# Hyena bias added as one-row matmuls, imaginary filter spectra before real ones, filter norm split around the first spectrum

## The chip, the cores and the metric

One core of one Trainium2 chip runs the whole kernel. The metric is the device time of one execution in microseconds (us); lower is better. The engines are TensorE (PE; its weight loads are PEld), VectorE (DVE), ScalarE (ACT), GpSimd (POOL) and SyncE (SP), which here only issues DMAs.

## What is computed

A transformer-like layer over 1024 latent tokens and 256 context tokens of width 1024: modulation from a condition vector, a joint input projection, three mixers side by side (Hyena long convolution, neighbourhood attention, RG-LRU), an output projection and a SwiGLU feed-forward block. The change touches only how the Hyena filters are prepared:

```python
h = jnp.sin(f_freq[0] * (z @ f_w1 + f_b1))
h = jnp.sin(f_freq[1] * (h @ f_w2 + f_b2))
k = (h @ f_w3).reshape(L, 2, 2, HY_WIDTH) * jnp.exp(-t * deltas)
k_circ = jnp.concatenate([kf, zeros, kb[:0:-1]], axis=0)
k_circ = k_circ / jnp.sum(jnp.abs(k_circ), axis=0, keepdims=True)
k_f = jnp.fft.rfft(k_circ, axis=0)
...
z = gate * (fft_conv(z, k_f[:, n]) + hy_bias[n] * z)
```

The bias term `hy_bias * z` is the same as adding a constant to every real value of the filter's spectrum, or adding it to the filter's tap at time 0.

## The kernel before

All products are made at close to full float32 precision from three passes over rounded halves: head of the weights times head of the data (`w_hi`, `eo_hi`), head times rest (`eo_lo`) and rest times head (`w_lo`). A head is a copy to the type f32r (ACT), a rest is a subtraction (POOL, some on DVE).

**Taps.** The filter is held as 8 tiles (`TILE[0..7]`, the first is tile 0) of even and odd parts, 128 x 2 x 512 each, in `eo`. For each pair of tiles PE multiplies (`taps`, L1942), DVE applies the decay (`window_taps`, L1342), ACT takes absolute values into `kabs` (L771) and makes the head of the tile (`filter_head`, L762), DVE takes the larger of the even and odd part (`larger`, L1328, into `kmax`), PE sums that over all taps into bank 5 (`filter_norm`, L2029; two records each), and POOL or DVE makes the rest (L1167, `tap_rest` L1334: DVE has the rests at positions 1, 3 and 5 of `SPLIT`, which are `TILE[2]`, `TILE[4]` and `TILE[6]`). Tile 0 needs a repair of its first row first (`efix`, L1355 and L1356, signal `k_fix`), and has its head and rest last.

**Bias.** When all eight norms are in bank 5, DVE multiplies the bias row by the norm (L1376), adds it to the first row of tile 0 (L1377, signal `k_bias`) and forms the row `nrow` of the norm for the later scaling (L1378, signal `nrow_ok`). Only then does ACT make the head of tile 0 and POOL its rest.

**Spectra.** `spectrum(n)`, n = 0 to 7, multiplies a table of cosines (n even: real part) or sines (n odd: imaginary part) with all 8 tiles, 24 matmuls of 128x512 in the order of `SPLIT`: heads (L1958), tap rests (L1967), table rests (L1974); for n = 0 the last two are exchanged. The table chunk n comes from memory by `k_raw(n)` (L522) into one of two `raw` buffers, ACT makes its head (`k_head(n)`, L754), POOL its rest (`k_rest(n)`, L1154). The result leaves by `spectrum_copy` (ACT, L810), `spectrum_out` (DVE, L1423) and `spectrum_store` (SP, L548).

**What lies between them.** PE also does `mod_sums(0..3)` (L1999, the modulation, whose weights `ada` are four loads of 2 MB), `norm_columns` (L1991, four tiny matmuls on `nrow`), `mod_columns` (L2007) and, from before `spectrum(3)` on, `turn_input` (L2020), the transposes of the normalised tokens. ACT squares the token tiles (`mean_square(n)`, L724), each of which is loaded by ACT's own DMA queue into `xstat`, three buffers deep: `mean_square(n)` issues the load of tile n + 3 (L717). It scales the tokens by their norm (`normalise(n)`, L796), which wants the rx values made from all ten squares.

Every engine runs one list of instructions, written out by hand in its block, with semaphores between them. SP's list in this part is: small loads, `k_raw(0)`, `k_raw(1)`, the four `ada` loads (L527), the bias table of the attention written through memory (`rpad` L529 and L531, sixteen copies to `rskew` L534), `k_raw(2)`, six token tiles (L540), `k_raw(3)`, `spectrum_store(0)` and so on. ACT's list around the point in question is `spectrum_copy(1)`, `k_head(3)`, `normalise(0..3)`, `spectrum_copy(2)`.

Of the kernel before, what the change touches and what calls it, by code (L numbers as in the profile page):

```python
# [17 lines left out]
F32 = mybir.dt.float32  # L18
F32R = mybir.dt.float32r
# [5 lines left out]
P = 128  # L25
# [23 lines left out]
RAD = 8  # L49
TAPS = ((0, 0), (1, 2), (1, 0), (1, 3), (1, 1), (0, 3), (0, 1), (0, 2))  # L50
TILE = tuple(4 * par + i for par, i in TAPS)
SPLIT = tuple(k for k in TILE if k) + (0,)
DVE_SPLIT = (1, 3, 5)
TURNS = ((0, 2), (2, 6), (6, 10))
PLUS, MINUS = (0, 7, 1, 6), (4, 3, 5, 2)
GU_JOBS, DOWN_JOBS = 2 * FT, 24
# [105 lines left out]
def program(nc, A, out):  # L162
    ctx = ExitStack()
    with ctx:
        base = 16512

        def at(name, off, shape, dt=F32):
            return nc.alloc_sbuf_tensor_at(name, [P] + list(shape), dt, offset=base + off)
# [29 lines left out]
        efix = at("efix", H_ + 20480, [2 * HY])  # L198
        nrow = efix
        kmax = [at(f"kmax{r}", a, [2 * HY]) for r, a in enumerate((H_ + 22528, H_ + 24576, H_ + 8192))]  # L200
        kabs = [at("kabs0", H_, [2, 2 * HY]), at("kabs1", H_ + 4096, [2, 2 * HY])]
        arow = at("arow", H_ + 26624, [2, HALF])
        zf = at("zf", H_, [SEQ])
# [258 lines left out]
        def _(sp):  # L462
# [55 lines left out]
            def k_raw(n):  # L518

                if n >= 2:  # L520
                    sp.wait_ge(klo, n - 1)
                sp.dma_start(raw[:, n % 2, :], A["ktab"][:, n * SEQ:(n + 1) * SEQ]).then_inc(kraw_ld[n % 2], 16)  # L522

            k_raw(0)
            k_raw(1)
# [15 lines left out]

            def spectrum_store(n):

                m, ri = n // 2, n % 2
                sp.wait_ge(kv_ok, n + 1)
                for side, j in enumerate((PLUS[m], MINUS[m])):
                    for o in range(2):
                        sp.dma_start(spec[o, j, :, ri, :], kev[:, n % 2, side, o * HY:(o + 1) * HY]).then_inc(ks_out[n % 2], 16)  # L548
# [149 lines left out]
        def _(act):  # L698
# [20 lines left out]
            def mean_square(n):  # L719

                if n:
                    act.wait_ge(x_sq, n)
                act.wait_ge(xs_ld[n % 3], 16 * (n // 3 + 1))
                act.activation(xstat[n % 3][:], xstat[n % 3][:], ACT.Square, accum_out=ssq[:, n:n + 1]).then_inc(x_sq, 1)  # L724
                if n + 3 < len(TILES):
                    act.wait_ge(x_sq, n + 1)
                    stats_dma(n + 3)
# [21 lines left out]
            def k_head(n):  # L749

                act.wait_ge(kraw_ld[n % 2], 16 * (n // 2 + 1))
                if n >= 2:
                    act.wait_ge(kjob, n - 1)
                act.activation(w_hi[:, n % 2, :], raw[:, n % 2, :], ACT.Copy).then_inc(khi, 1)  # L754

            k_head(0)
            mean_square(0)
            mean_square(1)

            def filter_head(k):  # L760

                act.activation(eo_hi[:, k].rearrange("p x c -> p (x c)"), eo[:, k].rearrange("p x c -> p (x c)"), ACT.Copy).then_inc(e_hi, 1)  # L762

            for t in range(RAD):
                if t:
                    act.wait_ge(k_eo, 4 * (t // 2) + 3 + t % 2)
                else:
                    act.wait_ge(k_fix, 1)
                if t >= 2:
                    act.wait_ge(k_max, t - 1)  # L770
                act.activation(kabs[t % 2][:], eo[:, TILE[t]], ACT.Abs).then_inc(k_abs, 1)  # L771
                if TILE[t]:
                    filter_head(TILE[t])
            k_head(1)
            mean_square(2)
            mean_square(3)

# [27 lines left out]
            def spectrum_copy(n):  # L805

                act.wait_ge(kjob, n + 1)
                if n:
                    act.wait_ge(kv_rd, n)
                act.activation(ktmp[:], ps[:, 2 * (n % 2), :], ACT.Copy).then_inc(kc_ok, 1)  # L810

            act.wait_ge(k_bias, 1)
            filter_head(0)
            mod_rows(0)
            mod_rows(1)
            mean_square(4)
            mean_square(5)
            mean_square(6)
            spectrum_copy(0)
            k_head(2)  # L820
            mean_square(7)
# [301 lines left out]
        def _(pool):  # L1123
# [25 lines left out]
            def k_rest(n):  # L1149

                pool.wait_ge(khi, n + 1)
                if n >= 2:
                    pool.wait_ge(kjob, n - 1)
                pool.tensor_tensor(w_lo[:, n % 2, :], raw[:, n % 2, :], w_hi[:, n % 2, :].bitcast(F32), ALU.subtract).then_inc(klo, 1)  # L1154
# [6 lines left out]
                    pool.tensor_tensor(ha_lo[:, k, a * P:z * P], xm[:, k, a * P:z * P], ha_hi[:, k, a * P:z * P].bitcast(F32),  # L1161
                                       ALU.subtract).then_inc(x_lo, 1)

            for n, k in enumerate(SPLIT):
                if n not in DVE_SPLIT:
                    pool.wait_ge(e_hi, n + 1)
                    pool.tensor_tensor(eo_lo[:, k].rearrange("p x c -> p (x c)"), eo[:, k].rearrange("p x c -> p (x c)"),  # L1167
                                       eo_hi[:, k].bitcast(F32).rearrange("p x c -> p (x c)"), ALU.subtract).then_inc(e_lo, 1)
                if n in (3, 6):
                    k_rest(n // 6)  # L1170
            k_rest(2)
            k_rest(3)
            k_rest(4)
# [85 lines left out]
        def _(dve):  # L1259
# [69 lines left out]

            def tap_rest(n):  # L1330

                k = SPLIT[n]
                dve.wait_ge(e_hi, n + 1)
                dve.tensor_tensor(eo_lo[:, k].rearrange("p x c -> p (x c)"), eo[:, k].rearrange("p x c -> p (x c)"),  # L1334
                                  eo_hi[:, k].bitcast(F32).rearrange("p x c -> p (x c)"), ALU.subtract).then_inc(e_lod, 1)
# [27 lines left out]
            for p in range(1, RAD // 2):  # L1363
                window_taps(p, 0)
                larger(2 * p - 2)
                window_taps(p, 1)
                larger(2 * p - 1)
                if p >= 2:
                    tap_rest(2 * p - 3)
            larger(RAD - 2)  # L1370
            larger(RAD - 1)
            tap_rest(5)

            dve.wait_ge(k_acc, RAD)
            dve.wait_ge(par_ld, 16 * 17)
            link(dve.tensor_tensor(hrow[0:1, :], hrow[0:1, :], ps[0:1, 5, :], ALU.mult))  # L1376
            dve.tensor_tensor(eo[0:1, 0], eo[0:1, 0], hrow[0:1, :].unsqueeze(1).broadcast_to([1, 2, 2 * HY]), ALU.add).then_inc(k_bias, 1)  # L1377
            dve.tensor_scalar(nrow[0:1, :], ps[0:1, 5, :], float(SEQ), None, ALU.mult).then_inc(nrow_ok, 1)  # L1378

            def lam_series():  # L1380
# [44 lines left out]
                dve.nop().then_inc(kv_rd, 1)  # L1425
                dve.nop().then_inc(kv_ok, 1)

            lam_series()
            filter_scale()
            spectrum_out(0)  # L1430
            dve.wait_ge(x_sq, 10)
            dve.tensor_scalar(rx[:], ssq[:], 1.0 / D, EPS, ALU.mult, ALU.add).then_inc(x_rs, 1)
            dve.wait_ge(x_sqrt, 1)
# [467 lines left out]
        def _(pe):  # L1901
# [43 lines left out]

            def spectrum(n):

                x = n % 2
                pe.wait_ge(khi, n + 1)
                if n >= 2:  # L1950
                    pe.wait_ge(kv_rd, n - 1)
                bank = lambda k: ps[:, 2 * x + k // 4, :]

                def heads():
                    for i, k in enumerate(SPLIT):
                        if n == 0:
                            pe.wait_ge(e_hi, i + 1)
                        pe.matmul(bank(k), w_hi[:, x, k * P:(k + 1) * P], eo_hi[:, k, x, :], start=k in (SPLIT[0], SPLIT[4]), stop=False)  # L1958

                def tap_rests(last):  # L1960
                    for i, k in enumerate(SPLIT):
                        if n == 0:
                            if i in DVE_SPLIT:
                                pe.wait_ge(e_lod, DVE_SPLIT.index(i) + 1)
                            else:
                                pe.wait_ge(e_lo, i + 1 - sum(d < i for d in DVE_SPLIT))
                        ins = pe.matmul(bank(k), w_hi[:, x, k * P:(k + 1) * P], eo_lo[:, k, x, :], start=False,  # L1967
                                        stop=last and k in (SPLIT[3], SPLIT[7]))
                    return ins

                def table_rests(last):
                    pe.wait_ge(klo, n + 1)
                    for k in SPLIT:
                        ins = pe.matmul(bank(k), w_lo[:, x, k * P:(k + 1) * P], eo_hi[:, k, x, :], start=False,  # L1974
                                        stop=last and k in (SPLIT[3], SPLIT[7]))
                    return ins

                heads()
                if n == 0:
                    table_rests(False)  # L1980
                    ins = tap_rests(True)
                else:
                    tap_rests(False)
                    ins = table_rests(True)
                ins.then_inc(kjob, 1)
# [45 lines left out]
            for p in range(RAD // 2):  # L2031
                taps(p, 0)
                taps(p, 1)
                if p >= 2:
                    filter_norm(2 * p - 4)
                    filter_norm(2 * p - 3)
            for t in range(RAD - 4, RAD):
                filter_norm(t)
            pe.wait_ge(sil_ok, 1)
            mod_sums(0)  # L2040
            mod_sums(1)
            spectrum(0)
            norm_columns()
            mod_columns(0)
            mod_columns(1)
# [353 lines left out]
```

## Time and profile before

| | us |
|---|---|
| median of 3 runs | 1478.46 (1477.99 to 1478.96) |
| profiled execution, own time | 1482.41 |
| its span | 1480.4 |
| mean granted TensorE clock in it | 0.984 |

The profiled execution is some 4 us longer than the median of the others. Busy time is counted per engine; a PE that is busy nearly all the span sets the time wherever it has no hole, and what counts for this change are the first 118 us, where PE still waits for other engines and for DMAs.

### The profile page before, as it was taken

The numbers are of one execution on the slowest core, as the hardware profiler recorded it, in microseconds if no ns is written. First come the engines' busy times: TensorE is split into PE (matmuls) and PEld (weight loads), VectorE is DVE, ScalarE is ACT, GpSimd is POOL, SyncE is SP. The second block draws the span as 40 slices with busy tenths as digits, with TensorE's granted clock in tenths as the row PEclk, the third lists the DMA queues.
The fourth block names the chain that finished last, engine by engine and source line by source line (L and its number), as shares of the span: only waits on it lengthen the run. The fifth ranks groups of instructions, "written<-read, shape, count | busy, mean of one in ns | idle before, by whom it ended". The sixth has DMA issues, their size and how long they took to land.

```text
span 1480.4 us, 20446 instructions
## 1 busy us (share of the span) xinstructions
PE 1413.7 (95%) x7737; PEld 1156.2 (78%) x7737; DVE 724.8 (49%) x1022; ACT 550.1 (37%) x861; POOL 608.2 (41%) x291
## 2 busy tenths in 40 slices
PE   5989999999998999999999999999999999999997
PEld 1579667899986888778678888878877888887886
DVE  7664557893936887448875111133356121110122
ACT  4572543322315777634322222222222222223222
POOL 2362112160426553474344444444443444443442
PEclk9999999999999999999999999999999999999999
DMA  9762101414104545432323333333323433332332
GB/s 335 256 221 60 40 29 40 132 32 140 45 27 112 142 131 145 143 98 87 127 78 93 96 98 90 99 89 93 102 86 110 117 99 92 99 92 79 93 96 89
DMA packets 236447, 156.63 MB, mean 106 GB/s; under 512 B 10531, under 2 KB 221873, under 8 KB 236251
## 3 DMA queue, kind: packets, MB, share of 16 engines
q1 hardware_dynamic: 234387, 148.70, 33.2%
q10 hardware_dynamic: 1992, 6.99, 1.4%
q8 instruction: 46, 0.75, 0.2%
q14 instruction: 22, 0.18, 0.0%
HBM read 147.25 MB, written 8.81 MB: 105 GB/s over the span
## 4 chain that ended last, share of the span: by engine, by line
PE 81%; DVE 9%; SPq 3%; ACT 2%; DMA 2%; issue 2%; POOL 1%; DVEq 0%; ACTq 0%
PE ps L1909 33%; PE ps L1914 17%; PE ps L2070 11%; PE ps L2073 5%; PE ps L2230 2%; PE ps L2207 2%; PE ps L2168 2%; PE ps L2086 1%; SPq L527 1%; DMA rpad<-zpad 1%; PE ps L2115 1%; PE ps L2127 1%; DMA raw<-in_ktab 1%; PE ps L2210 1%; POOL hb_lo L1226 1%
## 5 line engine op out<-in xcount | busy, mean ns | idle before, releaser
L1127 POOL TENSOR_TENSOR w_lo<-raw,w_hi 128x1024 fp32r<-128x1024 f32 x152 | 371.4, 2443 | 473.1 <-ACT w_hi L704 473.1
L1909 PE MATMUL ps<-hb_hi,w_hi 128*128 128x512 f32 x768 | 303.8, 396 | 10.1 <-DVE g_t L1812 5.4
L1909 PE MATMUL ps<-hb_lo,w_hi 128*128 128x512 f32 x768 | 301.9, 393 | 0.0
L704 ACT ACTIVATE w_hi<-raw 128x1024 fp32r<-128x1024 f32 x152 | 160.1, 1053 | 178.5 <-PE ps L1914 171.6
L1914 PE MATMUL ps<-hb_hi,w_lo 128*128 128x512 f32 x768 | 194.0, 395 | 0.0
L1147 POOL TENSOR_TENSOR w_lo<-raw,w_hi 128x1024 fp32r<-128x1024 f32 x21 | 88.1, 4197 | 226.6 <-ACT w_hi L860 226.6
L1909 PEld LDWEIGHTS ps<-hb_hi,w_hi 128*128 128x128 f32 x768 | 145.7, 190 | 44.6 <-DVE hb_lo L1777 7.6
L1914 PEld LDWEIGHTS ps<-hb_hi,w_lo 128*128 128x128 f32 x768 | 145.9, 190 | 32.7 <-issue 2.5
L1909 PEld LDWEIGHTS ps<-hb_lo,w_hi 128*128 128x128 f32 x768 | 146.0, 190 | 29.8
L2070 PE MATMUL ps<-ha_hi,w_hi 128*128 128x512 f32 (+2 forms) x432 | 164.2, 380 | 3.7 <-ACT w_hi L860 3.4
L2070 PE MATMUL ps<-ha_lo,w_hi 128*128 128x512 f32 (+2 forms) x432 | 161.6, 374 | 0.0
L1909 PE MATMUL ps<-a_hi,w_hi 128*128 128x512 f32 x352 | 138.0, 392 | 2.0 <-ACT w_hi L704 2.0
L1909 PE MATMUL ps<-a_lo,w_hi 128*128 128x512 f32 x352 | 137.2, 390 | 0.0
L1075 ACT ACTIVATE a_hi<-a_f 128x512 f32 (+1 forms) x44 | 27.8, 632 | 209.4 <-DVEq L1817 209.4
L1815 DVE SCALAR_TENSOR_TENSOR a_f<-g_t,ps 128x512 f32<-128x512 f32 x44 | 30.2, 688 | 149.8 <-PE ps L1914 149.6
L2073 PE MATMUL ps<-ha_hi,w_lo 128*128 128x512 f32 (+2 forms) x432 | 98.9, 371 | 0.0
L2070 PEld LDWEIGHTS ps<-ha_hi,w_hi 128*128 128x128 f32 x432 | 82.1, 190 | 17.8 <-issue 7.0
L1812 DVE SCALAR_TENSOR_TENSOR g_t<-g_t,ps 128x512 f32<-128x512 f32 x44 | 30.3, 688 | 125.8 <-ACT g_t L1071 125.1
L2070 PEld LDWEIGHTS ps<-ha_lo,w_hi 128*128 128x128 f32 x432 | 82.1, 190 | 10.2
L2073 PEld LDWEIGHTS ps<-ha_hi,w_lo 128*128 128x128 f32 x432 | 80.1, 188 | 10.1
L1914 PE MATMUL ps<-a_hi,w_lo 128*128 128x512 f32 x352 | 87.6, 389 | 0.0
L1909 PEld LDWEIGHTS ps<-a_hi,w_hi 128*128 128x128 f32 x352 | 66.2, 188 | 16.4 <-ACT w_hi L704 2.8
(279 smaller groups left out, 2088.1 us busy)
## 6 DMA issues: line engine op xcount, KB each, us to landing
raw<-in_ffn_w_gu SPq DMA_DIRECT2D x88, 512.0 KB, 3.8
ada1x<-in_ada_w SPq DMA_DIRECT2D x32, 512.0 KB, 3.9
raw<-in_ffn_w_down SPq DMA_DIRECT2D x32, 512.0 KB, 4.1
raw<-in_w_in SPq DMA_DIRECT2D x22, 512.0 KB, 4.0
ada<-in_ada_w SPq DMA_DIRECT2D x4, 2048.0 KB, 21.9
raw<-in_w_out SPq DMA_DIRECT2D x16, 512.0 KB, 4.2
raw<-in_ffn_w_down SPq DMA_DIRECT2D x16, 384.0 KB, 3.5
raw<-in_ktab SPq DMA_DIRECT2D x8, 512.0 KB, 6.4
```

What stands on the lines that cost most here:

```text
L704: act.activation(w_hi[:, b, :], raw[:, b, :], ACT.Copy).then_inc(hi_done, 1)
L1127: pool.tensor_tensor(w_lo[:, b, :], raw[:, b, :], w_hi[:, b, :].bitcast(F32), ALU.subtract).then_inc(lo_done, 1)
L1147: pool.tensor_tensor(w_lo[:, b, :], raw[:, b, :], w_hi[:, b, :].bitcast(F32), ALU.subtract).then_inc(llo, 1)
L1812: dve.scalar_tensor_tensor(g_t[:], g_t[:], 1.0, ps[:, 0, :], ALU.add, ALU.mult).then_inc(acc_free, 1)
L1815: dve.scalar_tensor_tensor(a_f[:], g_t[:], 0.5, ps[:, 1, :], ALU.mult, ALU.mult).then_inc(acc_free, 1)
L1909: pe.matmul(dst, w_hi[:, b, k * P:(k + 1) * P], x, start=start and i_ == 0 and n == 0, stop=False)
L1914: ins = pe.matmul(dst, w_lo[:, b, k * P:(k + 1) * P], rhs(k)[0], start=False, stop=stop and k == nk - 1)
L2070: pe.matmul(dst, w_hi[:, b, k * P:(k + 1) * P], x[:, k, a:z], start=k == 0 and n == 0, stop=False)
L2073: ins = pe.matmul(dst, w_lo[:, b, k * P:(k + 1) * P], ha_hi[:, k, a:z], start=False, stop=k == KT - 1)
L2168: ins = pe.matmul(dst, q_[hh, 4 * rb + cb, :], rhs, start=i == 0, stop=i == 2)
L2207: pe.transpose(ps[0:m, 4 + e, c * P:(c + 1) * P], pr[:, b, e, a:a + m], ident[:])
L2230: ins = pe.matmul(ps[hh, 7, 0:P], vtm[0:m, hp, tile, hh], pT[0:m, b, e, c, :], start=c == 0, stop=c == 4)
```

## The change

The bias is no longer added to tile 0. Instead DVE splits the row bias x norm into a head and a rest (`hb_row`), and each real spectrum gets two extra matmuls with a one-row stationary operand of ones (`one_row`) and these rows. The imaginary spectra, which have no bias, come first within the pairs (`PART`): n = 0, 2, 4, 7 are imaginary, n = 1, 3, 5, 6 real. Tile 0 is treated in turn with the others. The norms of the last two tiles are summed behind `spectrum(0)`, those of tiles 4 and 5 between `mod_sums(0)` and `mod_sums(1)`. POOL makes the two first table rests ahead of all tap rests; DVE makes its three tap rests behind the last decay; ACT makes `k_head(1)` early; `mean_square(4..6)` no longer stand behind the wait for `k_bias`; `lam_series` (27 small DVE operations) stands behind `spectrum_out(0)`.

```diff
-SPLIT = tuple(k for k in TILE if k) + (0,)
-DVE_SPLIT = (1, 3, 5)
+DVE_SPLIT = (2, 4, 6)
+PART = (1, 0, 1, 0, 1, 0, 0, 1)
@@ SP, k_raw(n) and spectrum_store(n)
-                sp.dma_start(raw[:, n % 2, :], A["ktab"][:, n * SEQ:(n + 1) * SEQ]).then_inc(kraw_ld[n % 2], 16)
+                sp.dma_start(raw[:, n % 2, :], A["ktab"][:, (n - n % 2 + PART[n]) * SEQ:(n - n % 2 + PART[n] + 1) * SEQ]).then_inc(kraw_ld[n % 2], 16)
-                m, ri = n // 2, n % 2
+                m, ri = n // 2, PART[n]
@@ ACT
             k_head(0)
+            k_head(1)
             mean_square(0)
             mean_square(1)
...
-                if TILE[t]:
-                    filter_head(TILE[t])
-            k_head(1)
+                filter_head(TILE[t])
             mean_square(2)
             mean_square(3)
...
-            act.wait_ge(k_bias, 1)
-            filter_head(0)
             mod_rows(0)
             mod_rows(1)
             mean_square(4)
             mean_square(5)
             mean_square(6)
+            act.wait_ge(k_bias, 1)
             spectrum_copy(0)
@@ POOL
-            for n, k in enumerate(SPLIT):
+            k_rest(0)
+            k_rest(1)
+            for n, k in enumerate(TILE):
                 if n not in DVE_SPLIT:
...
-                if n in (3, 6):
-                    k_rest(n // 6)
@@ DVE
-                if p >= 2:
-                    tap_rest(2 * p - 3)
+            tap_rest(2)
             larger(RAD - 2)
+            tap_rest(4)
             larger(RAD - 1)
-            tap_rest(5)
-
+            tap_rest(6)
+
+            dve.wait_ge(k_eo, 4 * RAD // 2)
+            link(dve.tensor_copy(one_row[0:1, :], ones[0:1, :]))
             dve.wait_ge(k_acc, RAD)
             dve.wait_ge(par_ld, 16 * 17)
             link(dve.tensor_tensor(hrow[0:1, :], hrow[0:1, :], ps[0:1, 5, :], ALU.mult))
-            dve.tensor_tensor(eo[0:1, 0], eo[0:1, 0], hrow[0:1, :].unsqueeze(1).broadcast_to([1, 2, 2 * HY]), ALU.add).then_inc(k_bias, 1)
+            link(dve.tensor_copy(hb_row[0][0:1, :], hrow[0:1, :]))
+            dve.tensor_tensor(hb_row[1][0:1, :], hrow[0:1, :], hb_row[0][0:1, :].bitcast(F32), ALU.subtract).then_inc(k_bias, 1)
...
-            lam_series()
             filter_scale()
             spectrum_out(0)
+            lam_series()
@@ PE, spectrum(n); all of its loops run over TILE in place of SPLIT
+                    if r == 0:
+                        pe.wait_ge(k_bias, 1)
+                        for row in hb_row:
+                            pe.matmul(bank(0), one_row[0:1, :], row[0:1, :], start=False, stop=False)
@@ PE, its list
-            for t in range(RAD - 4, RAD):
-                filter_norm(t)
             pe.wait_ge(sil_ok, 1)
             mod_sums(0)
+            filter_norm(RAD - 4)
+            filter_norm(RAD - 3)
             mod_sums(1)
+            pe.wait_ge(k_eo, 2 * RAD)
             spectrum(0)
+            filter_norm(RAD - 2)
+            filter_norm(RAD - 1)
             norm_columns()
```

## Rows read from the trace of the kernel before

**Rows 1.** The page: the span of the profiled execution

```profile
span 1480.4 us, 20446 instructions
```

**Rows 2.** The chain that ended last: start, length, what (us)

```profile
27.45 15.53 DMA rpad<-zpad
...
45.25 0.63 SPq L534
...
56.39 0.46 SPq L522
...
60.81 13.73 DMA raw<-in_ktab
...
105.17 2.03 issue
```

**Rows 3.** Timeline of PE: start, length, line, tiles, shape, count, idle before

```profile
33.45 2.15 PE L2029 MATMUL ps<-kmax,ones 128*128 128x512 f32 x4
40.52 6.84 PE L2029 MATMUL ps<-kmax,ones 128*128 128x512 f32 x8 [4.93 <-DVE kmax L1328]
47.30 3.64 PE L1999 MATMUL ps<-ada,silp 128*32 128x512 f32 x32
50.87 2.33 PE L1958 MATMUL ps<-eo_hi,w_hi 128*128 128x512 f32 x8
...
56.79 0.40 PE L1991 MATMUL ps<-ident,efix 1*128 1x1 f32 x4
57.12 1.95 PE L2007 MATMUL ps<-selc,arow 128*128 128x2 f32 x16
...
73.62 1.98 PE L1974 MATMUL ps<-eo_hi,w_lo 128*128 128x512 f32 x8
77.84 1.06 PE L2020 MATMUL ps<-ident,xin 128*128 128x128 f32 x8 [2.24 <-ACT xin L796]
...
109.57 3.03 PE L1958 MATMUL ps<-eo_hi,w_hi 128*128 128x512 f32 x8
```

**Rows 4.** Timeline of ACT and of its DMA queue (ACTq)

```profile
42.07 1.04 ACT L762 ACTIVATE eo_hi<-eo 128x1024 fp32r<-128x1024 f32 x1
...
54.68 0.33 ACTq L717 DMA_DIRECT2D xstat<-in_x  x1
...
74.56 1.06 ACT L754 ACTIVATE w_hi<-raw 128x1024 fp32r<-128x1024 f32 x1 [3.80 <-DMA raw<-in_ktab]
75.52 4.25 ACT L796 ACTIVATE xin<-xin,rx 128x1024 f32<-128x1024 f32 x4
...
90.76 0.60 ACT L810 ACTIVATE ktmp<-ps 128x512 f32<-128x512 f32 x1
```

**Rows 5.** DMAs from 56 to 76 us, ACT's queue: packets, MB, share

```profile
q10 hardware_dynamic: 419, 1.52, 22.6%
```

**Rows 6.** Windows: PE, PEld, DVE, ACT, POOL busy, PEclk, DMA share, GB/s

```profile
42.00:44.00 2.00, 2.00 (x3) 0.50 (x2) 2.00 (x3) 2.00 (x4) 0.00 (x0) 0.50 0.02 6
...
72.00:74.00 2.00, 2.00 (x10) 1.65 (x9) 0.61 (x4) 0.00 (x0) 0.00 (x0) 1.00 1.05 381
...
108.00:110.00 2.00, 2.00 (x12) 2.00 (x11) 1.75 (x4) 0.54 (x2) 1.39 (x1) 0.55 0.03 12
```

**Rows 7.** Timeline of DVE in the taps and behind them

```profile
21.92 0.67 DVE L1355 TENSOR_TENSOR efix<-eo 1x512 f32<-1x512 f32 x1
...
27.02 2.31 DVE L1328 TENSOR_TENSOR kmax<-kabs 128x512 f32<-128x512 f32 x1
...
34.34 3.38 DVE L1334 TENSOR_TENSOR eo_lo<-eo,eo_hi 128x1024 fp32r<-128x1024 f32 x1
...
41.59 0.68 DVE L1328 TENSOR_TENSOR kmax<-kabs 128x512 f32<-128x512 f32 x1
...
47.40 0.68 DVE L1376 TENSOR_TENSOR hrow<-hrow,ps 1x512 f32<-1x512 f32 x1 [1.49 <-PE ps L2029]
```

**Rows 8.** Timeline of POOL, 15 to 49 us

```profile
26.42 2.36 POOL L1167 TENSOR_TENSOR eo_lo<-eo,eo_hi 128x1024 fp32r<-128x1024 f32 x1 [24.45 <-ACT eo_hi L762]
```

More of the change, by code:

```diff
@@ L200, in program @@
         kmax = [at(f"kmax{r}", a, [2 * HY]) for r, a in enumerate((H_ + 22528, H_ + 24576, H_ + 8192))]
+        hb_row = [at("hb_row0", H_ + 8192, [2 * HY], F32R), at("hb_row1", H_ + 3072, [2 * HY], F32R)]
+        one_row = at("one_row", H_ + 18432, [P], F32R)
         kabs = [at("kabs0", H_, [2, 2 * HY]), at("kabs1", H_ + 4096, [2, 2 * HY])]
@@ L1330, in tap_rest @@
             def tap_rest(n):
-                k = SPLIT[n]
+                k = TILE[n]
                 dve.wait_ge(e_hi, n + 1)
@@ L1946, in spectrum @@
             def spectrum(n):
-                x = n % 2
+                x, r = n % 2, PART[n]
                 pe.wait_ge(khi, n + 1)
@@ L1954, in heads @@
                 def heads():
-                    for i, k in enumerate(SPLIT):
+                    for i, k in enumerate(TILE):
                         if n == 0:
                             pe.wait_ge(e_hi, i + 1)
-                        pe.matmul(bank(k), w_hi[:, x, k * P:(k + 1) * P], eo_hi[:, k, x, :], start=k in (SPLIT[0], SPLIT[4]), stop=False)
+                        pe.matmul(bank(k), w_hi[:, x, k * P:(k + 1) * P], eo_hi[:, k, r, :], start=i < 2, stop=False)
+                    if r == 0:
+                        pe.wait_ge(k_bias, 1)
+                        for row in hb_row:
+                            pe.matmul(bank(0), one_row[0:1, :], row[0:1, :], start=False, stop=False)
                 def tap_rests(last):
-                    for i, k in enumerate(SPLIT):
+                    for i, k in enumerate(TILE):
                         if n == 0:
@@ L1966, in tap_rests @@
                                 pe.wait_ge(e_lo, i + 1 - sum(d < i for d in DVE_SPLIT))
-                        ins = pe.matmul(bank(k), w_hi[:, x, k * P:(k + 1) * P], eo_lo[:, k, x, :], start=False,
-                                        stop=last and k in (SPLIT[3], SPLIT[7]))
+                        ins = pe.matmul(bank(k), w_hi[:, x, k * P:(k + 1) * P], eo_lo[:, k, r, :], start=False,
+                                        stop=last and k in (TILE[4], TILE[7]))
                     return ins
@@ L1972, in table_rests @@
                     pe.wait_ge(klo, n + 1)
-                    for k in SPLIT:
-                        ins = pe.matmul(bank(k), w_lo[:, x, k * P:(k + 1) * P], eo_hi[:, k, x, :], start=False,
-                                        stop=last and k in (SPLIT[3], SPLIT[7]))
+                    for k in TILE:
+                        ins = pe.matmul(bank(k), w_lo[:, x, k * P:(k + 1) * P], eo_hi[:, k, r, :], start=False,
+                                        stop=last and k in (TILE[4], TILE[7]))
                     return ins
```

## The prediction

> **What bounds the kernel now.** I read the page first for the span [rows 1], then the chain of waits, which says what released the work at each moment, then the timelines of PE, ACT and DVE over the first 118 us, and last the DMA windows. From the chain [rows 2] the reader is to see that the early part hangs on SP's queue: the write of `zpad` lands only at 42.98 us (behind the `ada` loads), sixteen copies of about 0.6 us each are issued from 45.25 on, so `k_raw(2)` goes out at 56.39 and `k_raw(3)` at 60.81. That chunk needs until 74.5 to land; then ACT does `k_head(3)` and, behind it in its list, `normalise(0)` and `(1)` [rows 4]: 74.56 + 0.96 + 2 x 1.06 = 77.6, and PE's first transpose starts at 77.84. I call that moment T. PE's timeline [rows 3] is a second chain into T: from the two `mod_sums` at 47.30 it has no hole until `spectrum(2)` ends at 75.60, and it waits 2.24 us there. Behind T PE runs without a hole to 105.17 and waits 2.03 us for ACT [rows 2]. All that follows is started by progress of the kernel, not by a fixed time, so what T gains is carried to the end, unless the hole at 105 us gives or takes something.
>
> So T is the later of two times: PE's, with 2.24 us to spare, and that of the DMA. Both have to move for a gain.
>
> **PE's chain.** The start S of `spectrum(0)` is 50.87 now [rows 3]. After the change there stand directly before it `filter_norm(5)` and `mod_sums(1)`; the norms of tiles 6 and 7 come behind. A norm is 2.15 / 2 = 1.08 us, a `mod_sums` 3.64 / 2 = 1.82 [rows 3]. The start is set by `larger(5)`, which ends at 41.59 + 0.68 = 42.3 now [rows 7]. In front of it goes the tap rest of 3.38 us. Against this come: the head of tile 0 on ACT, 0.95 us from start to start (rows like the head of another tile, 1.04 busy [rows 4]); its rest on POOL, 2.36 [rows 8]; and the two table rests of the same length, which POOL does from the end of `k_head(0)`, about 19.3, to about 24.1. The rows say that this is not free: a `kmax` operation beside a POOL rest takes 2.31 where one alone takes 0.68, and it ends when the POOL operation ends (26.42 + 2.36 = 28.78, plus 0.68 is 29.4) [rows 7, 8]. `efix`, at 21.92 now [rows 7], would thus end at about 24.7, 2 us later, and so would `k_fix` and the first absolute values. Following the alternation DVE, ACT, POOL for all eight tiles with these durations, and with each two-input DVE operation held until the POOL operation beside it ends, I get the end of `larger(5)` at 41.7: three rests on POOL collide with a `larger` each, and the 3.38 us that leave DVE pay for it. Bounds: 39 (no collision) to 44 (each collision 1 us worse).
>
> (The Trainium skill, SBUF — State Buffer, section SBUF: two separate sides, says that VectorE with two SBUF inputs and GpSimd take one pair of ports as an exclusive lock for a whole instruction. By that rule, which speaks against moving the table rests ahead, the collisions are whole operations, as the trace shows with 2.31 against 0.68; without the lock `larger(5)` would end near 39.)
>
> S = 41.7 + 1.08 + 1.82 = 44.6. `spectrum(0)` takes 56.79 - 50.87 = 5.92, so it ends at 50.5; its last tap rest (DVE, about 48.1) is then there. The other two norms: 52.7. Now there is a new wait: `norm_columns` needs `nrow`, and DVE forms that only now, by the product (0.68 [rows 7]), a copy of the row (the trace has no such one; between 0.35, half of that, and 0.68; I take 0.5), a subtraction and the norm row (0.68 each): 2.6 with the gaps. POOL rests in this time. So `norm_columns` starts at 55.3 against 56.79: of the 6.3 us that S gains, 1.5 are left. From there to the end of `spectrum(2)` it is 75.60 - 56.79 = 18.8 now; `spectrum(1)` is real and gets two more matmuls. Their price: 1.98 us for 8 [rows 3], thus 0.25 each, 0.5 together. A one-row f32r matmul of 512 columns is not in the trace; from below it is nothing, from above that of a norm, 1.08. PE is ready for T at 55.3 + 18.8 + 0.5 = 74.6 (76.9 with `larger(5)` at its upper bound, which makes 1478.0; at its lower one the DMA side decides).
>
> `lam_series` moves from in front of `spectrum_out(0)` to behind it. It takes about 7 us, would run from 58.5 to 66, and the ACT square it precedes is done at about 66.6: hidden. With that cover gone it would delay `normalise`, by at most 1 us.
>
> **The DMA side.** SP's issue times do not move: the waits for `zpad` and for sixteen issues are untouched, and what `k_raw(2)`, the token tiles and `k_raw(3)` wait for is earlier anyway. What moves are the loads of `xstat` tiles 7, 8 and 9 on ACT's queue. The first is issued at 54.68 and the others 1.6 us apart, because `mean_square(4..6)` stand behind `k_bias`; all 1.52 MB of them pass after 56 us [rows 4, 5], in the stretch in which the DMA engines are full (share 1.05 with 381 GB/s at 72 to 74 [rows 6]). After the change ACT makes the last absolute value and head from 41.7 to 43.6, does two squares with their loads (1.8 us each) and two row copies (0.5 each) to 48.4, and issues the three loads at about 50, 51.8 and 53.5, before `k_raw(2)`. What comes before chunk 3 is 8 x 0.524 = 4.2 MB on SP's queue. Taking 1.2 to 1.5 MB away at 0.39 MB per us saves 3.1 to 3.9 us: chunk 3 lands at 70.6 to 71.4. T by this side is 3.3 later, 73.9 to 74.7. ACT itself is ready: it stood idle for 3.80 us before `k_head(3)` for this load alone [rows 4], and what it does before that starts no later than now.
>
> So T goes from 77.84 to about 74.7: 3.1 us.
>
> **Behind T.** Real spectra n = 3, 5 and 6 have 0.5 us more each. That of n = 3 delays `spectrum(4)` and so `spectrum_copy(4)` at 90.76, which ACT takes up the moment PE ends; ACT had 0.1 to 0.2 us of slack there, so 0.3 us goes on the path. Those of n = 5 and 6 fall into the 2.03 us hole, where ACT is late and not PE: cost nothing, and 1.0 us each with the other if that hole were not there. Sum: 3.1 - 0.3 = 2.8. The sum is against the profiled time of 1482.41; the median of the runs lies 3.95 lower, and I take the same difference from it: 1478.46 - 2.8 = 1475.7. Adding a part for the chance that the hole at 105 us stops costing clock (below), I would shade to 1475.4; as the likeliest case I give 1475.5.
>
> **The rivals.**
>
> *Clock lost in the new hole.* From 52.7 to about 57.4 PE would do nothing but tiny matmuls. After the hole of 4.93 us before 40.52 [rows 3] the granted clock is 0.50 (42 to 44), after that at 105 it is 0.55 (108 to 110) [rows 6]. If it falls here, the next two `mod_sums` run at 1.2 GHz; at the second fall `spectrum(7)`'s heads took 3.03 for about 2.1 [rows 3], and with the transposes before them 1.8 us went. The same here: PE ready at 76.3, gain 1.2, time 1477.3. For it: the hole is of the length that did it; against: the matmuls at 57.12 [rows 3] were preceded by no fall now. (The Trainium skill, TensorE: Matmul & The Clock Gate, section HAM oscillation, warns that an idle array drops to half clock and pays to come back. By that rule, with which the row at 108 us agrees, this rival would be the rule and not the exception.) Chance 0.2.
>
> *Clock regained at 105 us.* PE is 1 us later against ACT there, so the hole shrinks from 2.03 to about 1.1. If the clock then stays, the 1.8 us come on top: 1475.5 - 1.8 = 1473.7. Chance 0.22.
>
> *The chunk does not land earlier, and it ends slower.* If `xstat` is not what holds chunk 3, T stays at 77.84 and PE, ready at 74.6, stands idle for 3.3 instead of 2.24 us. Then 0.3 is lost for n = 3, and if the clock falls in that longer hole, `spectrum(3)` loses 1.8: 1478.8 to 1480.6. It decides from a landing later than 74.2. For it: three more requests queue behind chunk 3 in that stretch and may share the engines with it; against: 1.52 MB at 0.39 per us is 3.9 us, which has to go somewhere. Chance 0.13.
>
> *My likeliest case*, 1475.5, own range 1474.5 to 1477: chance 0.45.
>
> **How the numbers follow.** A measurement of this kernel can tell about 0.2%, 3.0 us, from no change; the bound for faster is 1475.5, in the middle of the likeliest case. Faster: 0.22 + 0.26 of 0.45 = 0.48. Same: 0.19 + 0.20 + 0.03 = 0.42. Slower: 0.10. The range runs from 1472.9 (regained clock, with the collisions at their lower bound) to 1479.0, and leaves out the part of the slower rival in which the clock falls, and more than one gain together.
>
> **What the new profile would show.** `spectrum(0)` starting at 44 to 46 and `norm_columns` at 55 to 56; a PE hole of 2.6 us before it; `xstat` issues before 54; `k_head(3)` starting at 70.5 to 71.5; the first transpose at 74 to 75.5; `spectrum(7)`'s heads 3.0 or 2.1 us long. The prediction is wrong if `k_head(3)` still starts at 74.5, if one-row matmuls take 1 us, or if the clock reads 0.5 between 56 and 66 us.

## The result, and the profile after

| | us |
|---|---|
| changed kernel, median of 12 runs | 1482.45 (1480.93 to 1484.17) |
| kernel before, median of 12 runs beside them | 1478.62 (1476.67 to 1479.79) |
| ratio, with 95% interval | 1.0028 [1.0019, 1.0037] |
| profiled execution of the changed kernel, own time / span | 1483.53 / 1481.7 |

The change makes the kernel slower by 0.2 to 0.4%, some 4 us. I had forecast 3 us in the other direction. The page [rows 1]:

```profile
span 1481.7 us, 20465 instructions
```

PE's timeline after, with the columns of [rows 3]:

```profile
45.12 2.11 PE L1961 MATMUL ps<-eo_hi,w_hi 128*128 128x512 f32 x8
...
50.69 1.88 PE L2036 MATMUL ps<-kmax,ones 128*128 128x512 f32 x4
55.16 0.48 PE L1998 MATMUL ps<-ident,efix 1*128 1x1 f32 x4 [2.59 <-DVE efix L1381]
55.56 3.58 PE L2014 MATMUL ps<-selc,arow 128*128 128x2 f32 x16
59.07 5.15 PE L2006 MATMUL ps<-ada,silp 128*32 128x512 f32 x32
64.15 2.10 PE L1961 MATMUL ps<-eo_hi,w_hi 128*128 128x512 f32 x8
66.19 0.73 PE L1965 MATMUL ps<-hb_row,one_row 1*128 1x512 f32 x2
66.85 2.09 PE L1974 MATMUL ps<-eo_lo,w_hi 128*128 128x512 f32 x8
...
77.89 1.04 PE L2027 MATMUL ps<-ident,xin 128*128 128x128 f32 x8
...
85.09 1.04 PE L2027 MATMUL ps<-ident,xin 128*128 128x128 f32 x8
```

Up to the fourth row I read what I had forecast: `spectrum(0)` at 45.12 (44.6), a wait of 2.59 us (2.6), `norm_columns` at 55.16 (55.3). Then comes the loss: the sixteen matmuls of `mod_columns` take 3.58 us where they took 1.95 [rows 3], and the 32 of `mod_sums` 5.15 where they took 3.64. T, the first transpose, is at 77.89 and no longer waits for ACT: PE itself is late. The last row, the next transposes, serves to price the one-row matmuls further down. The windows show the clock (columns as in [rows 6]):

```profile
54.00:56.00 2.00, 0.84 (x6) 0.83 (x7) 1.10 (x2) 0.60 (x1) 0.00 (x0) 0.84 0.98 273
...
60.00:62.00 2.00, 2.00 (x16) 0.51 (x12) 1.66 (x11) 0.65 (x1) 0.00 (x0) 0.50 0.92 375
...
108.00:110.00 2.00, 2.00 (x19) 1.92 (x17) 1.31 (x3) 1.35 (x2) 0.57 (x1) 1.00 0.00 0
```

The granted clock falls about when the wait ends (the 0.84 of the first row means some 0.6 us at half clock before 56) and stands at 0.50, that is 1.2 GHz, past 62 us, for 6.8 us in all; at 108 us it is 1.00 where [rows 6] had 0.55. The chain that ended last now holds neither SP nor a DMA here, as [rows 2] did, but DVE and PE (start, length, what):

```profile
49.12 3.55 issue
52.66 0.69 DVE hrow L1378
...
59.14 5.08 PE ps L2006 x32
```

ACT's timeline answers to [rows 4]. The loads of `xstat` are issued at 49.52 and 53.02 (first and last of three), and `k_head(3)` at 71.28 waited for no chunk: ACT stood idle until PE had ended `spectrum(1)`, copied that, and went on.

```profile
49.52 0.33 ACTq L719 DMA_DIRECT2D xstat<-in_x  x1
...
70.79 0.60 ACT L811 ACTIVATE ktmp<-ps 128x512 f32<-128x512 f32 x1 [2.15 <-PE ps L1981]
71.28 1.05 ACT L756 ACTIVATE w_hi<-raw 128x1024 fp32r<-128x1024 f32 x1
```

From 56 to 76 us ACT's queue moved this, for the 1.52 MB of [rows 5]:

```profile
q10 hardware_dynamic: 101, 0.35, 4.3%
```

DVE's timeline, beside [rows 7], shows the collisions. POOL's two table rests ran from 20.19 to 24.87 (last row; POOL's own timeline), beside the first of DVE's two operations.

```profile
22.65 2.76 DVE L1355 TENSOR_TENSOR efix<-eo 1x512 f32<-1x512 f32 x1
...
39.98 2.17 DVE L1328 TENSOR_TENSOR kmax<-kabs 128x512 f32<-128x512 f32 x1
```

```profile
20.19 4.68 POOL L1154 TENSOR_TENSOR w_lo<-raw,w_hi 128x1024 fp32r<-128x1024 f32 x2 [18.21 <-ACT w_hi L756]
```

### The profile page after: what moved, and what is told of

Same layout as the page of the kernel before. It is cut to its first block, busy times and chain, and to the rows that moved or that the text cites. A ratio compares the mean times of both kernels' runs of the same rounds, so it can differ in the third digit from the quotient of the medians.

```text
span 1481.7 us, 20465 instructions
## 1 busy us (share of the span) xinstructions
PE 1417.4 (96%) x7745; PEld 1157.1 (78%) x7745; DVE 728.2 (49%) x1024; ACT 550.2 (37%) x861; POOL 607.6 (41%) x291
## 4 chain that ended last, share of the span: by engine, by line
PE 81%; DVE 12%; ACT 3%; issue 2%; POOL 1%; DMA 0%; ACTq 0%; DVEq 0%
PE ps L1912 32%; PE ps L1917 16%; PE ps L2080 11%; PE ps L2083 5%; PE ps L2240 2%; PE ps L2178 1%; PE ps L2217 1%; PE ps L2096 1%; ACT pr L995 1%; PE ps L2137 1%; PE ps L2125 1%; DVE a_f L1748 1%; PE ps L1974 1%; PE ps L1961 1%; PE ps L1981 1%
## 5 line engine op out<-in xcount | busy, mean ns | idle before, releaser
L2080 PEld LDWEIGHTS ps<-ha_hi,w_hi 128*128 128x128 f32 x432 | 82.8, 192 | 18.1 <-issue 7.0
```

The source lines that it names most:

```text
L2080: pe.matmul(dst, w_hi[:, b, k * P:(k + 1) * P], x[:, k, a:z], start=k == 0 and n == 0, stop=False)
```

## The experiments

Two theories stood at the start. **Clock:** the new wait costs the granted clock, and that costs more than the norms' move gains. **Baseline:** the 3.1 us that T was to gain were a property of one profile. Two rivals: POOL's table rests in front of the taps cost the time, or the one-row matmuls do. Each time is the median of twelve runs, given against the median of the kernel before timed beside them (35 or 22 runs); only the two profiles of experiment 2 are one run each. Warm means at a granted clock of 1.00, cold at 0.50.

**1. The kernel before, unchanged.**

> The kernel before, unchanged, for a second profile and more times. Theory A (the changed kernel loses because its own PE chain grew: clock fall behind the new hole, and one-row matmuls): this profile looks like the first, k_head(3) at 74.5 and first transpose at 77.8. Theory B (the first profile of before was an unusually slow execution, 4 us over the median, and showed the load of table chunk 3 later than it usually lands): k_head(3) starts 1 to 3 us earlier here, the first transpose at 75.7 to 77, the span near 1477.

1480.09 against 1479.98, ratio 1.0009 [0.9997, 1.0021]. Its span is 1476.0, and its profile differs from the one I had read. ACT, then PE:

```profile
72.27 1.06 ACT L754 ACTIVATE w_hi<-raw 128x1024 fp32r<-128x1024 f32 x1 [1.63 <-DMA raw<-in_ktab]
```

```profile
59.00 5.34 PE L1999 MATMUL ps<-ada,silp 128*32 128x512 f32 x32
...
77.13 1.03 PE L2020 MATMUL ps<-ident,xin 128*128 128x128 f32 x8
...
83.47 1.04 PE L2020 MATMUL ps<-ident,xin 128*128 128x128 f32 x8
...
105.77 0.41 PE L2020 MATMUL ps<-ident,xin 128*128 128x128 f32 x2 [1.34 <-issue]
```

Chunk 3 was there 2.3 us sooner than in [rows 4], T had no wait for ACT in front of it, and `mod_sums` shows the clock fall (5.34 for 3.64) that I thought absent before.

**2. Two more profiles of the kernel before.**

> The kernel before, unchanged, a third profile. Theory B (the first profile showed the load of table chunk 3 later than usual): k_head(3) starts at 70 to 73, the first transpose at 75.7 (PE ready, warm clock) to 77.2 (clock fall at 59 us), the projection at 113.7 to 115.3. If the first profile was the rule: 74.5, 77.8 and 116.5 to 118.3.

> The kernel before, unchanged, a fourth profile; expectations as for the third.

1479.63 and 1478.01, spans 1477.6 and 1475.9. The first of them had its `mod_sums` warm, and T with it:

```profile
59.40 3.64 PE L1999 MATMUL ps<-ada,silp 128*32 128x512 f32 x32
...
75.84 1.03 PE L2020 MATMUL ps<-ident,xin 128*128 128x128 f32 x8
```

The second is like experiment 1, with 5.34 and T at 77.08. So T of the kernel before is 75.84 with a warm `mod_sums` and 77.1 with a cold one, set by PE both times. The 77.84 and the 2.24 us of waiting in [rows 3] came in one profile of four. So did the slow stretch at 105 us: from T to the first matmul of the projection it took 40.5 us there and 38.1 in the three others. Of these 2.4 us, 0.7 is a longer wait (2.03 us for 1.34) and some 1.6 are slow clock behind it.

**3. Chunk 3 asked for earlier, in the kernel before.** This moves the DMA side alone.

```diff
                 x_dma(n)
+            k_raw(3)
             sp.wait_ge(ada_mm, 2)
...
             x_dma(5)
-            k_raw(3)
             spectrum_store(0)
```

> The kernel before with k_raw(3) issued ahead of the token tiles 4 and 5. If the load of chunk 3 holds the first transpose in before as the first profile shows (2.24 us of idle PE): 2.2 us faster than before, ratio 0.9985. Theory B (in the usual execution it lands in time): no change, ratio 1.000 within 0.0003.

1479.65 against 1479.98, ratio 1.0000 [0.9986, 1.0014]. T is at 75.84, and ACT's row is this:

```profile
69.54 1.05 ACT L754 ACTIVATE w_hi<-raw 128x1024 fp32r<-128x1024 f32 x1
```

`k_head(3)` is 1.8 to 3.3 us earlier than in experiments 1 and 2, and T is where PE's chain puts it: `mod_sums` start at 57.70 and T follows 18.1 us later, as in experiment 1 (59.00 and 77.13). So an earlier chunk gains nothing at T in this profile. The whole profile runs 1.1 us ahead of that of experiment 1 from the start of the taps on, which makes its T as early as the 75.84 above. The times alone say less: the twelve fall in two groups of six, at 1475.8 to 1478.4 and at 1480.9 to 1482.9, and the interval only just excludes the 2.2 us that I had set as the other outcome.

**4. The norms of the last two tiles back in front of `spectrum(0)`.** The row for DVE is then made under `spectrum(0)`.

```diff
-            spectrum(0)
             filter_norm(RAD - 2)
             filter_norm(RAD - 1)
+            spectrum(0)
             norm_columns()
```

> The changed kernel with the norms of tiles 6 and 7 summed ahead of spectrum(0) again. Theory A: spectrum(0) starts 3.9 us later (49.0) but norm_columns follow at once at 54.9 with a warm clock, so 3 us less up to mod_sums(3): 1479.3 to 1480. Theory C: no change, 1482.5.

1479.32 against 1479.98, ratio 0.9998 [0.9986, 1.0009]. PE:

```profile
46.87 1.12 PE L2036 MATMUL ps<-kmax,ones 128*128 128x512 f32 x2 [1.61 <-DVE kmax L1328]
...
53.39 0.40 PE L1998 MATMUL ps<-ident,efix 1*128 1x1 f32 x4
53.72 1.95 PE L2014 MATMUL ps<-selc,arow 128*128 128x2 f32 x16
55.60 3.64 PE L2006 MATMUL ps<-ada,silp 128*32 128x512 f32 x32
...
74.02 1.07 PE L2027 MATMUL ps<-ident,xin 128*128 128x128 f32 x8 [0.91 <-ACT xin L797]
```

`spectrum(0)` starts 2.3 us later than in the changed kernel (47.43), but everything behind it runs warm, and T is 3.9 us earlier. Of these, 1.0 belongs to the execution and not to the edit: DVE's first decay operation starts at 18.83 here and at 19.80 in the changed kernel.

**5. The wait filled by other work of the kernel.** `mod_sums(2)` and `mod_columns(0)` go ahead of `norm_columns`; `filter_scale` waits for the larger count.

```diff
             filter_norm(RAD - 1)
-            norm_columns()
+            mod_sums(2)
             mod_columns(0)
+            norm_columns()
             mod_columns(1)
-            mod_sums(2)
             mod_sums(3)
@@ DVE, filter_scale
-                dve.wait_ge(mod_done, 6)
+                dve.wait_ge(mod_done, 10)
```

> The changed kernel with mod_sums(2) and mod_columns(0) in the hole of PE behind the last two norms, norm_columns behind them. Theory A: the hole of 2.6 us and the clock fall go (3.1 us of longer tiny matmuls and mod_sums, and 2.6 of idle time); PE is ready for the first transpose at about 72.5, which then starts with the DMA side at about 74.4: 3 us faster than the changed kernel, 1479.3. If the hole costs nothing (theory C: it is the load that sets the start of the transposes, and the loss comes later): 1482.5, as the changed kernel.

1479.22 against 1479.98, ratio 1.0002 [0.9989, 1.0015]. Inside the time is dealt out otherwise: PE is early at T, waits there, and pays clock there. ACT, then PE:

```profile
73.12 1.06 ACT L756 ACTIVATE w_hi<-raw 128x1024 fp32r<-128x1024 f32 x1 [4.14 <-DMA raw<-in_ktab]
```

```profile
76.40 1.51 PE L2027 MATMUL ps<-ident,xin 128*128 128x128 f32 x8 [3.64 <-ACT xin L797]
77.56 3.35 PE L1961 MATMUL ps<-eo_hi,w_hi 128*128 128x512 f32 x8
```

From T to the projection this takes 41.0 us, for 39.3 in the changed kernel. It is what my slower rival described: chunk 3 lands at 73.1 and no sooner, PE is ready before it, and a longer hole before T has a clock fall behind it. What made the chunk late here is not shown.

**6. The changed kernel again, and without its bias rows.**

> The changed kernel again, beside the kernel before on the same chip. Theory A (the loss is the hole in PE behind the last two norms, with the clock fall behind it, plus 0.66 us for each pair of one-row matmuls on the path): about 2 to 4 us slower than before in the median, the profile with norm_columns at 55, the two stretches behind it taking 3.1 us longer than warm, and the input projection starting at 117 against 115.3 for an execution of before without a clock fall at 105. Theory D (the 4 us of the first comparison were in good part chance of where the clock falls in the later stages): ratio below 1.0015.

1482.49 against 1479.17, ratio 1.0018 [1.0006, 1.0030]; T at 79.02, span 1481.1. The loss is there again, smaller than the first time (3.3 us by medians for 3.8); the ratio's interval also holds 1.0015, so that part of the first 3.8 us may have been chance. PE, where `norm_columns` had waited 2.59 us as before:

```profile
56.54 2.62 PE L2014 MATMUL ps<-selc,arow 128*128 128x2 f32 x16
59.09 6.27 PE L2006 MATMUL ps<-ada,silp 128*32 128x512 f32 x32
```

The second edit takes the one-row matmuls out, so the kernel leaves the bias out of its result:

```diff
-                    if r == 0:
+                    if n == 1:
                         pe.wait_ge(k_bias, 1)
-                        for row in hb_row:
-                            pe.matmul(bank(0), one_row[0:1, :], row[0:1, :], start=False, stop=False)
```

> The changed kernel without the eight one-row matmuls, so the bias is left out of the filters. Theory A: 0.66 us less in each of the four real spectra, 2.6 us faster than the changed kernel if PE is what holds the path there; if ScalarE takes over behind it at the token tiles (as in before, where PE idles 1.3 to 2.0 us before the transposes of the last tiles), 1.3 to 2.

1480.21 against 1479.17, ratio 1.0006 [0.9996, 1.0017]: 2.3 us less than the changed kernel, by medians. PE:

```profile
55.48 0.40 PE L1996 MATMUL ps<-ident,efix 1*128 1x1 f32 x4 [2.59 <-DVE efix L1381]
55.81 1.95 PE L2012 MATMUL ps<-selc,arow 128*128 128x2 f32 x16
57.69 5.34 PE L2004 MATMUL ps<-ada,silp 128*32 128x512 f32 x32
...
75.82 1.03 PE L2025 MATMUL ps<-ident,xin 128*128 128x128 f32 x8
...
104.94 0.41 PE L2025 MATMUL ps<-ident,xin 128*128 128x128 f32 x2 [1.82 <-issue]
```

A wait of 1.82 us at 105 is there, and T to projection is 38.6 for 39.3. A pair of rows turns out to cost more than its own 0.66 us: from T to the next transposes PE takes 7.20 us in the changed kernel (77.89 to 85.09) and 6.34 without a pair in experiment 1 (77.13 to 83.47), so 0.86, as the matmuls beside the pair take longer too. T itself is 3.2 us earlier than in the changed kernel's profile just above. That is 0.9 for one pair, 0.7 for an earlier start of the taps (DVE's first decay at 20.12 for 20.82), and 1.6 for a shorter clock fall, which taking out the rows does not explain. I take 0.9 + 0.7 = 1.6 us as what this profile shows of the rows themselves. The clock fall matters for the main argument: the same wait of 2.59 us stands in front of `norm_columns` here, and it cost only 1.7 us (5.34 for 3.64).

**7. POOL's order as before.** The two table rests go back among the tap rests.

```diff
-            k_rest(0)
-            k_rest(1)
             for n, k in enumerate(TILE):
...
+                if n in (3, 6):
+                    k_rest(n // 6)
```

> The changed kernel with POOL's first two table rests back among the tap rests. Theory A: efix is no longer held for 2 us, spectrum(0) and all of PE's chain up to the first transpose come 1 to 2 us earlier, total 1 to 2 us faster than the changed kernel. If the collisions only change places: no change.

1482.33 against 1479.17, ratio 1.0019 [1.0008, 1.0030]: the loss is all there. PE, then DVE:

```profile
49.81 0.73 PE L1974 MATMUL ps<-eo_lo,w_hi 128*128 128x512 f32 x2 [0.81 <-DVE eo_lo L1334]
...
54.85 0.58 PE L1998 MATMUL ps<-ident,efix 1*128 1x1 f32 x4 [2.59 <-DVE efix L1381]
...
58.87 6.50 PE L2006 MATMUL ps<-ada,silp 128*32 128x512 f32 x32
```

```profile
22.87 0.67 DVE L1355 TENSOR_TENSOR efix<-eo 1x512 f32<-1x512 f32 x1
```

`efix` costs 0.67 again, not 2.76, and `spectrum(0)` starts at 43.72, 1.4 us sooner; but `norm_columns` is only 0.3 us sooner, since `spectrum(0)` now waits 0.81 us for DVE's last tap rest: the collisions have moved there (on DVE's timeline a tap rest at 40.68 takes 3.40 us for 1.21). The wait in front of `norm_columns` and the clock fall stay.

**8. DVE's row as late as ever, the array kept busy until it comes.** Ten matmuls of 128x512 whose result nobody reads stand between the last norms and `norm_columns`. DVE's row is made no earlier by them.

```diff
             filter_norm(RAD - 1)
+            pe.wait_ge(khi, 2)
+            for _ in range(10):
+                pe.matmul(ps[:, 2, :], w_hi[:, 1, 0:P], eo_hi[:, 0, 0, :], start=True, stop=True)
             norm_columns()
```

> The changed kernel with ten matmuls of 128x512 into an unused bank, placed in PE's hole between the last two norms and norm_columns; the wait for nrow stays. It separates the clock from the wait. Theory A: norm_columns start as before the edit (55 to 56), but the clock does not fall behind it, the sixteen tiny matmuls and two mod_sums take 1.95 and 3.64 us in place of 3.5 and 5.1, and the total is 2 to 3 us below the changed kernel, about that of before. If the wait for nrow is what costs: within 0.5 us of the changed kernel.

1479.65 against 1479.74, ratio 1.0000 [0.9988, 1.0012]. PE:

```profile
52.23 2.88 PE L2055 MATMUL ps<-eo_hi,w_hi 128*128 128x512 f32 x10
55.38 0.40 PE L1998 MATMUL ps<-ident,efix 1*128 1x1 f32 x4 [0.27 <-DVE efix L1381]
55.72 1.95 PE L2014 MATMUL ps<-selc,arow 128*128 128x2 f32 x16
57.59 5.34 PE L2006 MATMUL ps<-ada,silp 128*32 128x512 f32 x32
...
76.59 1.03 PE L2027 MATMUL ps<-ident,xin 128*128 128x128 f32 x8
```

This is the most direct of them. `norm_columns` starts 0.2 us later than in the changed kernel, nothing is taken away, 2.9 us of useless work are added, and the kernel is 2.8 us faster than the changed one by medians. The two were timed apart; their ratios to the kernel before differ by 0.0018, with intervals of 0.0012 to each side, so the gain is just clear of the noise and its size is not. `mod_columns` is warm; `mod_sums`, which I had expected warm too, still has the fall, as in two of the four profiles of the kernel before. The profile alone proves nothing, since experiment 6 shows the same 1.95 and 5.34 with the wait left empty: it is the twelve times that carry this experiment.

**9. What the runs point to.** The norms in front of `spectrum(0)`, DVE's `larger(7)` ahead of its last two tap rests, and chunk 3 asked for early (the edits of 3 and 4, and this):

```diff
             larger(RAD - 2)
-            tap_rest(4)
             larger(RAD - 1)
+            tap_rest(4)
             tap_rest(6)
```

> The changed kernel with the last two norms ahead of spectrum(0), the last larger() of DVE ahead of its last two tap rests, and k_raw(3) issued ahead of token tiles 4 and 5. Theory A: norm_columns at 52.5 to 53, first transpose at about 72.8, projection start at 112 to 112.5: 3 to 4 us faster than before, 1476.5 on the chip of the last runs. If a limit that the early profile does not show sets the total: within 1 us of before.

1477.32 against 1479.17, ratio 0.9986 [0.9974, 0.9999]; T at 73.23, span 1475.4. `norm_columns` wait for nothing, and still `mod_sums` have the fall:

```profile
54.24 5.34 PE L2006 MATMUL ps<-ada,silp 128*32 128x512 f32 x32
```

It beats the changed kernel, by 5 us, and the kernel before by a margin that its interval only just tells from nothing. Then the same with `mod_sums(3)` behind `spectrum(1)`, so that the small-operand matmuls don't stand in one block:

> The best version so far (norms ahead of spectrum(0), last larger() first, k_raw(3) early) with mod_sums(3) behind spectrum(1), so that the stretches of small matmuls are shorter. Theory A: no clock fall between 50 and 70 us; first transpose 72 to 72.5 in place of 73.2, total 0.5 to 1.5 us below that version. If mod_sums keep the clock up as well as full matmuls do: no change.

1478.00 against 1479.74, ratio 0.9993 [0.9980, 1.0005]. The cold half is there all the same (3.21 us for 16 matmuls, 1.92 warm), and T falls back to 75.76, since DVE's part of the modulation now comes late:

```profile
55.13 3.21 PE L2006 MATMUL ps<-ada,silp 128*32 128x512 f32 x16
...
75.76 0.44 PE L2027 MATMUL ps<-ident,xin 128*128 128x128 f32 x2 [1.19 <-DVEq L1445]
```

## Why the prediction was wrong

**PE's chain up to `norm_columns`: right.** `larger(5)` ended at 42.15 (41.7), `spectrum(0)` started at 45.12 (44.6), `norm_columns` at 55.16 (55.3). The collisions came in kind, if not in number: up to `larger(5)` four `kmax` operations were held where I had counted three, three of them some 1.65 us long and the one at 39.98 2.17, and `efix` took 2.76 and, in experiment 7, 0.67 with POOL's rest away from it. That the end came out within 0.5 us is in part luck. (The Trainium skill, SBUF — State Buffer, section SBUF: two separate sides, describes this lock of VectorE against GpSimd; these rows agree with it.) The table rests ahead of the taps cost no measured time all the same: 1.0019 against 1.0018.

**The clock: the step that failed first.** The sum that made PE ready at 74.6 held nothing for the clock; "Clock lost in the new hole" stood beside it as a rival, with a chance of 0.2 and a price of 1.8 us. It is what happened, and the sign that I had named for it, a clock of 0.5 between 56 and 66 us, is in the windows. In the profile after, it cost 3.58 - 1.95 = 1.6 us in `mod_columns` and 5.15 - 3.64 = 1.5 in `mod_sums`, 3.1 together, so PE was ready for T at 77.9 and not at 74.6. By the same two rows it cost 3.3 us in the second profile of the changed kernel, 4.5 in experiment 7 and 1.7 in experiment 6: four profiles with the wait, a fall in each, 3.2 us on average. The kernel before has no such wait and paid 0, 1.7, 0 and 1.7 us in its four profiles, so the net loss by clock is some 2.3 us. The argument against it, that [rows 3] show no fall at 57.12, was bad twice. There PE ran `spectrum(0)` up to the tiny matmuls, while now 2.59 us of nothing stand in front of them; and even without that wait two of four profiles of the kernel before show the fall in `mod_sums`.

That the empty wait is what makes the loss rests on the times of three experiments: 8 fills it and makes nothing else earlier, 4 and 5 remove it, and each ends at the kernel before (1.0000, 0.9998, 1.0002), while the two that keep it and all the work end at 1.0018 and 1.0019. It is not the whole of the clock's account, for the fall also comes without the wait (5.34 in experiments 1, 3 and 9 and in one profile of 2), and what decides between a fall of 1.7 us and one of 4.5 is open. (The Trainium skill, TensorE: Matmul & The Clock Gate, section HAM oscillation — how this bites in real kernels, describes an array that goes to half clock in its waits and starts the next matmuls cold. The trace agrees as far as all four profiles with the wait show the fall; it shows one without a wait too.)

**The baseline: the step that failed second.** "So T goes from 77.84 to about 74.7" took T from a profile that stood 4 us above the median, and then took the gain off that median. T in the other three profiles is 75.84, 77.13 and 77.08. I had written down the 3.95 us and moved on; a good part of them were this late T and the 2.4 us lost behind it, by a longer wait at 105 and the slow clock after it. The gain on the DMA side did not exist: `xstat`'s loads moved as forecast (0.35 MB for 1.52 after 56 us), and in the profile after chunk 3 no longer held `k_head(3)`; but in experiments 1 and 2 T did not hang on the chunk either. Nor does the chunk land 3.1 to 3.9 us sooner: where `k_head(3)` waits for it in the changed order (experiments 4, 5, 6 and 8) the wait ends at 70.6 to 73.1 us, in experiments 1 and 2 at 71.35 to 72.8. "Clock regained at 105 us" came true too, with `spectrum(7)`'s heads at 2.1 us and the window at 1.00; but the kernel before usually has that as well, so it is no gain.

**The one-row matmuls: mis-sized.** 0.66 us a pair for themselves (66.19 to 66.85) and 0.86 with what they cost their neighbours (experiment 6), not 0.5. And the cover for n = 5 and 6 was thinner than the profile's 2.03 us: T to projection takes 39.3 us for 38.1, 1.2 us lost where I had 0.3. The three pairs add 2.6 us to PE there, and the wait at 105, 1.34 us in experiment 1, is gone, which gives 1.3 back. Without the rows 0.7 of the 1.2 come back; the other 0.5 is the longer wait at 105 in experiment 6 (1.82 for 1.34), so ACT is later there for a reason that no run separates.

**The sum, made again.** Against the three usual profiles of the kernel before (mean T 76.7), the three with the changed order and all its work (the changed kernel twice, experiment 7) have a mean T of 78.65: 1.9 us. The terms give the same: `norm_columns` 1.5 us sooner, the clock 2.5 worse (3.6 for 1.1 in these profiles), a pair of rows 0.9. With 1.2 behind T that is 3.1 us at the projection. The measured differences are 3.8 and 3.3 us by the medians of the two comparisons. Of the 7 us between 1475.5 and 1482.45, the unpriced clock is 3.6, the late T of the one profile 1.1, and the rows 1.3; the rest, about 1, is in no term that I can name. (Two small slips in the prediction: its upper bound for `larger(5)` makes 1477.8 by its own terms, not 1478.0, and the slow clock at 105 us cost 1.6 us, not 1.8.) What comes after the projection is the same instructions in both and took 1360.7 to 1363.6 us before, 1362.8 to 1364.5 after. The means lie 1.8 us apart, with clock falls that come and go in short waits, and so few profiles don't say whether any of it belongs to the change.

**Why repairs only reach par.** Experiments 4, 5 and 8 all end within 0.05% of the kernel before. The changed order puts PE ahead in the taps, but bias rows (1.6 us) and the next late partner (ACT at T in 4 and 5, with chunk 3 behind it) take it back. Only with DVE's norm made sooner and chunk 3 early too (9) does some of it stay; which of the two does it was not taken apart.

## What to carry over

When work is deferred behind a stage, ask what small chain hangs on its result, and price the wait together with what the array runs right behind it: 2.6 us of waiting ahead of small matmuls came with 1.7 to 4.5 us of slow clock, where the order without it had 0 or 1.7. Let the producer of such a chain (here the norms) stand ahead of a long stage, so that the other engine works under cover; where that can't be, try filling the wait: ten full-size matmuls without a use were better here than leaving it empty. And before a slack of 2 us carries an argument, profile the baseline more than once, above all when the profile stands several us above the median.

## What the runs showed of the hardware

- Full-width matmuls that nobody needs made the kernel faster: 2.88 us of them in a wait saved 2.8 us by medians (1479.65 for 1482.49).
- The same 32 matmuls of `mod_sums` took 3.64, 5.15, 5.34, 6.27 or 6.50 us. The unchanged kernel before showed both 3.64 and 5.34 from one execution to the next, with PE busy without a hole up to them.
- A matmul with a one-row stationary operand costs more, not less, than a full one of 512 columns: 0.66 us a pair against 1.98 us for eight [rows 3]; 0.33 against 0.25 each. With what its neighbours lose a pair costs 0.86 us.
- The copy of one row of 512 elements took DVE 0.41 us, against 0.68 for two-input operations on such a row.
